# Compressed scores as transposed products, bias tables and sample rounds moved, all expert row dots from PSUM

## What is computed

```python
def dense_attn(q, k, v, q_pos, k_pos, slopes, window):
    s = jnp.einsum('...qgrd,...kgd->...grqk', q, k) * (B_HD ** -0.5)
    dist = q_pos[..., None, None, :, None] - k_pos[..., None, None, None, :]
    s = s - slopes[:, :, None, None] * dist
    p = jnp.where(mask, jax.nn.softmax(jnp.where(mask, s, NEG), axis=-1), 0.0)
    o = jnp.einsum('...grqk,...kgd->...qgrd', p, v)
    return o, p
...
    y_b = (g[:, :, 0] * o_cmp + g[:, :, 1] * o_slc + g[:, :, 2] * o_win)
...
def one(xb):                                   # peer_ffn, per token block
    ...
    top_s, j = lax.top_k(cand, P_TOPK)         # 8 heads, 16 of 16384 experts each
    eidx = jnp.take_along_axis(cidx, j, axis=-1)
    gate = jax.nn.softmax(top_s, axis=-1)
    u = peer_u[eidx]
    v = peer_v[eidx]
    act = jax.nn.gelu(jnp.einsum('td,tpkd->tpk', xb, u), approximate=False)
    return jnp.einsum('tpk,tpkd->td', gate * act, v)
```

## Time and profile before

| | us |
|---|---|
| median of 3 runs | 2270.77 |
| lowest and highest | 2267.69, 2270.86 |
| the profiled execution | 2268.58 |
| its span, first to last instruction | 2266.9 |

### The profile page before, as it was taken

How to read it: one execution, slowest core, us unless ns; L and a number is a source line. 1 busy time by engine, 2 the same in 40 slices (tenths; PEclk the granted TensorE clock), 3 DMA queues, 4 the chain that set the end, 5 groups by cost and what they waited for, 6 DMA issues and landing times.

```text
span 2266.9 us, 34232 instructions
## 1 busy us (share of the span) xinstructions
PE 2144.5 (95%) x13322; PEld 1893.3 (84%) x13322; DVE 1500.4 (66%) x3063; ACT 992.6 (44%) x1760; POOL 917.7 (40%) x608
## 2 busy tenths in 40 slices
PE   7999999988998999999989998999999999999998
PEld 7798988766555987999989998899997787888886
DVE  3334232345777545397889879975536989888886
ACT  2122322232777431333336665566543454454452
POOL 1000222311210000346866766677665554655530
PEclk9999999996999999999989999999999999999999
DMA  5234333346101543227879997999999999999993
GB/s 202 79 138 112 107 107 111 115 159 173 35 2 39 182 140 117 93 77 230 300 245 295 313 303 250 307 342 353 370 309 358 373 386 377 387 397 389 388 358 124
DMA packets 190233, 518.05 MB, mean 229 GB/s; under 512 B 15684, under 2 KB 85432, under 8 KB 185336
## 3 DMA queue, kind: packets, MB, share of 16 engines
q1 hardware_dynamic: 138648, 330.28, 41.7%
q0 software_dynamic: 50848, 184.53, 22.3%
q10 hardware_dynamic: 576, 1.05, 0.1%
HBM read 446.18 MB, written 73.75 MB: 229 GB/s over the span
## 4 chain that ended last, share of the span: by engine, by line
PE 46%; DVE 9%; DMA 3%; ACT 1%; issue 1%; SPq 0%; POOL 0%; DVEq 0%; ACTq 0%
PE ps_e L2439 22%; PE ps_e L2410 5%; PE ps_e L2411 5%; PE ps_e L2414 5%; DVE row L2760 3%; PE ps_e L2431 3%; DMA u_raw<-in_peer_uT 2%; PE ps_e L2463 1%; PE ps_e L2468 1%; PE ps_e L2469 1%; PE ps_e L2472 1%; PE ps_e L2399 1%; DMA e_gate<-gate_tables 1%; DVE one_a L2745 1%; DVE one_b L2745 1%
## 5 line engine op out<-in xcount | busy, mean ns | idle before, releaser
L2352 POOL DMA_INDIRECT row<-in_peer_v,sparse_idx x160 | 270.4, 1690 | 220.0 <-DVE y L2768 159.4
L2410 PE MATMUL ps_e<-hTh,u_hi 128*128 128x384 f32 x1024 | 358.1, 350 | 0.4 <-ACT gelu_out L2515 0.4
L2359 POOL TENSOR_TENSOR u_lo<-u_raw,u_hi 128x1024 fp32r<-128x1024 f32 x128 | 314.6, 2459 | 101.9 <-ACT u_hi L2509 99.1
L2411 PE MATMUL ps_e<-hTl,u_hi 128*128 128x384 f32 x1024 | 350.2, 342 | 0.0
L2439 PE MATMUL ps_e<-v_hi,w_hi 128*128 128x512 f32 x768 | 243.6, 399 | 5.5 <-DVE v_lo L2788 4.1
L2439 PE MATMUL ps_e<-v_lo,w_hi 128*128 128x512 f32 x768 | 241.5, 395 | 0.0
L2439 PE MATMUL ps_e<-v_hi,w_lo 128*128 128x512 f32 x768 | 241.4, 396 | 0.0
L2788 DVE TENSOR_TENSOR v_lo<-v_raw,v_hi 128x1024 fp32r<-128x1024 f32 x128 | 161.0, 1260 | 97.5 <-ACT v_hi L2548 97.5
L2414 PE MATMUL ps_e<-hTh,u_lo 128*128 128x384 f32 x1024 | 201.1, 338 | 0.5 <-POOL u_lo L2359 0.5
L2352 POOL DMA_INDIRECT row<-in_peer_u,sparse_idx x150 | 156.6, 1044 | 103.1 <-DVE sparse_hid L2760 79.7
L2410 PEld LDWEIGHTS ps_e<-hTh,u_hi 128*128 128x128 f32 x1024 | 196.8, 192 | 0.7 <-ACT u_hi L2509 0.7
(11 more groups left out here) (528 smaller groups left out, 4666.2 us busy)
## 6 DMA issues: line engine op xcount, KB each, us to landing
u_raw<-in_peer_uT SPq DMA_DIRECT2D x128, 512.0 KB
v_raw<-in_peer_v SPq DMA_DIRECT2D x32, 2048.0 KB, 10.2
hidden_gelu<-gelu_out SPq DMA_DIRECT2D x64, 384.0 KB
gate_tables<-g_buf SPq DMA_DIRECT2D x48, 512.0 KB
e_gate<-gate_tables SPq DMA_DIRECT2D x32, 768.0 KB, 13.1
gelu_in<-hidden_gelu SPq DMA_DIRECT2D x32, 768.0 KB, 16.2
w_raw<-in_w_tiles SPq DMA_DIRECT2D x45, 512.0 KB, 3.5
gw_raw<-in_merge_tiles SPq DMA_DIRECT2D x16, 512.0 KB, 4.4
```

Of the source, the lines that this page charges most:

```text
L2352: pool.indirect_dma_start(out=row[:, :], out_offset=None, in_=io.peer_u if i < U_END else io.peer_v, in_offset=bass.IndirectOffsetOnAxis(a ...
L2359: pool.tensor_tensor(u_lo[:, n % UB, :, :], u_raw[:, n % UB, :, :], u_hi[:, n % UB, :, :].bitcast(F32), ALU.subtract).then_inc(ul_done, 1)
L2410: pe.matmul(ps[:, n % 2, 0:TD], u_hi[:, n % UB, dc, :], hTh[:, dc, :], start=(dc == 0), stop=False)
L2411: pe.matmul(ps[:, n % 2, 0:TD], u_hi[:, n % UB, dc, :], hTl[:, dc, :], start=False, stop=False)
```

## The change

Attention. `dist`, the first two pairs' bias tables, `cdist` and `valid` are made by GpSimd in `stage_compress`, and the same lines go from `stage_attend`. The compressed scores are computed transposed: for each group g, 32 columns of a wider `kcB` (its two 8-key blocks and zeros) are the stationary operand and 512 queries move, two rounds (r) of four groups that write different partitions of bank 7; ScalarE copies the result to SBUF as `csT`, and TensorE transposes it back in four tiles. VectorE's softmax of them moves from units 0 and 1 to 1 and 2, the other small steps by a unit, and the gate terms behind `minima(0)`. Each sample item comes one pair earlier, and the splits of `Y_AT` come every second unit.

Experts. ScalarE copies `hp` into PSUM banks 4 and 5 at the end of round 57, SP then loads the 128 prompt tokens into the tile `hp`, ScalarE copies them back into the banks at the end of round 81, and all dots read PSUM. `row_due` is dealt out in three parts to fit.

```diff
@@ -1032,13 +1032,17 @@
...
-    s.kcB = at("kcB", 52960, [P, KV, 2, 8])
+    s.kcB = at("kcB", 14144, [P, 16 + KV * 32])
...
-    s.att = 36992
+    s.att = a0 = 36992
...
+    s.bias = at("abias", a0 + 512, [P, 2, 2, TP])
@@ -1106,6 +1110,24 @@
...
+
+            pool.iota(s.dist[:, :], pattern=[[-1, TP]], base=384, channel_multiplier=1,
+                      allow_small_or_imprecise_dtypes=True)
+
+            pool.iota(s.cdist[:, :, :], pattern=[[P, 4], [-CB, 8]], base=1 - CB, channel_multiplier=1,
+                      allow_small_or_imprecise_dtypes=True).then_inc(dist_made, 1)
+            pool.wait_ge(dist_made, 1)
+            pool.affine_select(out=s.dist[:, :], in_=s.dist[:, :], compare_op=ALU.is_ge, fill=BIG, base=384,
+                               pattern=[[-1, TP]], channel_multiplier=1).then_inc(dist_made, 1)
+            pool.affine_select(out=s.valid[:, :, :], in_=s.ones[:, 0:32].rearrange("p (i n) -> p i n", i=4),
+                               compare_op=ALU.is_ge, fill=0.0, base=1 - CB, pattern=[[P, 4], [-CB, 8]],
+                               channel_multiplier=1)
+            pool.affine_select(out=s.cdist[:, :, :], in_=s.cdist[:, :, :], compare_op=ALU.is_ge, fill=BIG, base=1 - CB,
+                               pattern=[[P, 4], [-CB, 8]], channel_multiplier=1)
+            pool.wait_ge(dist_made, 2)
+            for p in range(2):
+                for e in range(2):
+                    pool.tensor_scalar(s.bias[:, p, e, :], s.dist[:, :], SLOPES[2 * p + e], None, ALU.mult)
@@ -1179,8 +1201,9 @@
...
-            link(dve.tensor_scalar(s.kcB[0:HD, :, 0, :], src, pcol[0:HD, 0:1], None, ALU.add))
-            dve.tensor_copy(s.kcB[HD:P, :, 1, :], s.kcB[0:HD, :, 0, :])
+            keys = s.kcB[:, 16:16 + KV * 32].rearrange("p (g x) -> p g x", x=32)
+            link(dve.tensor_scalar(keys[0:HD, :, 0:8], src, pcol[0:HD, 0:1], None, ALU.add))
+            dve.tensor_copy(keys[HD:P, :, 8:16], keys[0:HD, :, 0:8])
@@ -1258,7 +1279,7 @@
...
-    items = [("p", 0), ("p", 1), ("p", 2), ("s", 0), ("p", 3), ("s", 1), ("p", 4), ("s", 2), ("p", 5), ("s", 3), ("p", 6), ("p", 7)]
+    items = [("p", 0), ("p", 1), ("s", 0), ("p", 2), ("s", 1), ("p", 3), ("s", 2), ("p", 4), ("s", 3), ("p", 5), ("p", 6), ("p", 7)]
@@ -1268,12 +1289,13 @@
...
-    Y_AT = [SMP_END + 4 + dc for dc in range(DC)]
+    Y_AT = [SMP_END + 4 + 2 * dc for dc in range(DC)]
...
+        chain = sem("att_chain")
...
+        csT_psum, csT_ready = sem("csT_psum"), sem("csT_ready")
@@ -1438,27 +1443,33 @@
...
             scores(1)
-            for i in range(4):
-                for p in range(NP):
-                    last = pe.matmul(ps[:, 7, i * P + 16 * p:i * P + 16 * (p + 1)], s.bqT[:, p, i * P:(i + 1) * P],
-                                     s.kcB[:, 2 * p // REP, :, :].rearrange("p e n -> p (e n)"), start=True, stop=True)
-            last.then_inc(cs_psum, 1)
+            for r in range(2):
+                for g in range(KV):
+                    c = 32 * g + 16 * (1 - r)
+                    last = pe.matmul(ps[32 * g:32 * g + 32, 7, :], s.kcB[:, c:c + 32], s.bqT[:, 2 * g + r, 0:TP],
+                                     start=(r == 0), stop=(r == 1))
+            last.then_inc(csT_psum, 1)
             for u in range(NU):
...
                     scores(u + 2)
+                if u == 0:
+                    pe.wait_ge(csT_ready, 1)
+                    for i in range(4):
+                        last = pe.transpose(ps[:, 7, i * P:(i + 1) * P], csT[:, i * P:(i + 1) * P], s.ident[:, :])
+                    last.then_inc(cs_psum, 1)
                 turn(u)
...
                         turn_rows(k)
-                if u == 3:
+                if u == 4:
                     pe.wait_ge(pc_ready, 1)
...
                     last.then_inc(pcT_psum, 1)
-                if u == 5:
+                if u == 6:
                     pe.wait_ge(sel_ready, 2)
@@ -1476,10 +1487,11 @@
...
-            dve.wait_ge(gate_exp, 1)
-            dve.tensor_scalar(s.gden[:, 0:4, :], s.gden[:, 0:4, :], 1.0, None, ALU.add)
-            dve.tensor_scalar(s.gden[0:TS, 4, :], s.gden[0:TS, 4, :], 1.0, None, ALU.add).then_inc(gden_ready, 1)
-            dve.wait_ge(gden_ready, 1)
+            def gate_terms():
+                dve.wait_ge(gate_exp, 1)
+                dve.tensor_scalar(s.gden[:, 0:4, :], s.gden[:, 0:4, :], 1.0, None, ALU.add)
+                dve.tensor_scalar(s.gden[0:TS, 4, :], s.gden[0:TS, 4, :], 1.0, None, ALU.add).then_inc(gden_ready, 1)
+                dve.wait_ge(gden_ready, 1)
@@ -1570,24 +1581,25 @@
...
             minima(0)
+            gate_terms()
             for u in range(NU):
...
                 scale(u)
-                if u == 0:
+                if u == 1:
                     compressed_scores()
-                if u == 1:
+                if u == 2:
                     compressed_shares()
...
                     masked_values(12, BH)
-                if u == 4:
+                if u == 5:
                     dve.wait_ge(pcT_psum, 1)
                     dve.tensor_copy(pcT[:, :], ps[:, 7, :]).then_inc(pcT_ready, 1)
-                if u == 5:
+                if u == 4:
                     masked_values(6, 12)
...
                     masked_values(0, 6).then_inc(vbd_ready, 1)
-                if u == 7:
+                if u == 8:
                     gate_sums()
@@ -1659,9 +1671,12 @@
...
                 exponentials(u)
+                if u == 0:
+                    act.wait_ge(csT_psum, 1)
+                    act.copy(csT[:, :], ps[:, 7, :]).then_inc(csT_ready, 1)
                 if u >= 1:
                     copy_turned(u - 1)
-                if u == 1:
+                if u == 2:
                     act.wait_ge(cexp_in, 1)
@@ -2173,8 +2188,11 @@
...
-    row_due = ([0] * PRE + [30 + i * 52 / 68 for i in range(68)]
-               + [82 + i * 36 / (U_END - PRE - 68) for i in range(U_END - PRE - 68)]
+    PACK_AT, H3_AT = 57, 81
+    LAST3 = HALF3 + NSP
+    row_due = ([0] * PRE + [30 + i * 25 / (HALF3 - PRE) for i in range(HALF3 - PRE)]
+               + [PACK_AT + 1 + i * 21 / NSP for i in range(NSP)]
+               + [H3_AT + 1 + i * 36 / (U_END - LAST3) for i in range(U_END - LAST3)]
@@ -2280,6 +2298,10 @@
...
                                  gbuf[b % 2][:, gs, :, :].rearrange("p g t j -> p g (t j)")).then_inc(g_sent[b % 2], 16)
+                if n == PACK_AT + 2:
+
+                    sp.wait_ge(h3_ready, 2)
+                    sp.dma_start(hp[:, :], io.h_rows[TD:TP, :]).then_inc(h3_in, 16)
                 if n == V_AT:
@@ -2622,6 +2644,14 @@
...
                     gate_copy(q)
+                if n == PACK_AT:
+                    act.wait_ge(hp_in, 16 * 4)
+                    act.wait_ge(rows_done, HALF3)
+                    act.copy(ps[:, 4:6, :], hp[:, :].rearrange("p (a b) -> p a b", a=2)).then_inc(h3_ready, 1)
+                if n == H3_AT:
+                    act.wait_ge(h3_in, 32)
+                    act.wait_ge(rows_done, LAST3)
+                    act.copy(ps[:, 4:6, :], hp[:, :].rearrange("p (a b) -> p a b", a=2)).then_inc(h3_ready, 1)
                 if n == GP_AT:
@@ -2755,9 +2785,10 @@
...
                     if i == HALF3:
-                        dve.wait_ge(hp_in, 16 * 4)
-                    token = ps[:, 4:6, :] if c < NS3 else hp[:, :].rearrange("p (a b) -> p a b", a=2)
-                    dve.tensor_tensor_reduce(out=row, in0=row, in1=token, scale=1.0, scalar=0.0, op0=ALU.mult,
+                        dve.wait_ge(h3_ready, 2)
+                    if i == LAST3:
+                        dve.wait_ge(h3_ready, 3)
+                    dve.tensor_tensor_reduce(out=row, in0=row, in1=ps[:, 4:6, :], scale=1.0, scalar=0.0, op0=ALU.mult,
                                              op1=ALU.add, accum_out=hid[:, c:c + 1]).then_inc(rows_done, 1)
...
                 dve.wait_ge(rows_done, i)
```

## The result

| us | before | after |
|---|---|---|
| median, lowest to highest (5 runs each) | 2270.77, 2267.04 to 2273.63 | 2256.99, 2245.25 to 2262.66 |
| ratio of the two, 95% interval | | 0.9938, 0.9909 to 0.9966 |
| the profiled execution, its span | 2268.58, 2266.9 | 2256.99, 2255.3 |

The kernel is faster by 13.8 us (0.6%). The forecast was 2252.0 with a range of 2240 to 2262. A second set of 12 runs of the same kernel, between fresh runs of before, gave 0.9953 (0.9937 to 0.9969), 11.8 us. So the gain fell short of the forecast 18.8 by 5 to 7 us; the median lies inside the stated range and 1 us above the 2248 to 2256 that the forecast called its own.

What follows compares the result with a forecast made beforehand. TensorE was taken as the bound, so edits pay only where it stands still or runs at low clock. Terms -7.0 - 2.0 - 9.8 = -18.8 us gave 2249.8 profiled, median 2252.0; range 2240 to 2262.

Steps and rivals of the forecast that it cites:

- Attention start: Start of the attention stage: early tables and transposed compressed scores bring the first turned tile forward, -7.0 us.
- the clock term: Attention start: 1.2 GHz lasting until 561 gives back up to 5 of 7.4 us; -7.0 taken.
- the bound of 10: Attention start: upper bound of the gain, -10 us, used for the clock rising early.
- the first rival: Attention start: the low clock eats the gain, -2.5 in place of -7.0 us, total 2256.5; chance 0.17.
- The second rival: Clock rises early at attention start (-10), wait near rounds 58 to 62 mostly goes (-7, with its clock): 2241; chance 0.15.
- Sample rounds: End of the attention stage: sample items a pair earlier let the splits spread, -2.0 us (bounds +1 and -5.3).
- at the earlier rate it would idle 1.8: Last 39 us of attention: TensorE idles 7.1 us, 1.8 at the earlier rate; less than half of 5.3 counted.
- First standstill: Expert hidden loop, rounds 58 to 62: VectorE ends `resolve` sooner with short dots, -2.6 us; half clock stays.
- Second standstill: Expert hidden loop, `resolve` of round 79: VectorE's lead covers it, -5.3 us, and -2.9 for the half clock.
- barrier: PSUM refills after rounds 57 and 81 drain the row pipeline: 2276 for both (chance 0.04), 2264 for one (0.05).
- DMA behind round 82: Rounds 82 to 118: three more rows, 1.6 MB, cost +1.0 us (bounds 0 and +4.4).
- the rival on DMA: From round 82 DMA takes over: +4.4 us and one more standstill with half clock (4.7 + 2.9), 2263; chance 0.08.

Runs made afterwards that it cites:

- part 3 alone: Kernel before with only the expert change (PSUM refills, all row dots from PSUM, new due rounds): 2257.86 us, ratio 0.9958.
- part 1 alone: Kernel before with only the transposed compressed scores and the early bias tables, items and splits as before: 2256.82 us, ratio 0.9952.

## Why the prediction was right, and which steps were not

The measured 13.8 us lie in the range partly because errors cancelled. By the stages of the two traces, attention gained 8.3 us where 9.0 were forecast (both parts), rounds 57 to 66 5.1 for 2.6, rounds 66 to 82 8.5 for 8.2, but rounds 82 to 127 lost 6.2 for 1.0 and rounds 30 to 57 4.3 for nothing.

**Attention start: right mechanism, gain too small, since the clock term was mis-sized.** From the timelines, with the time at 1.2 GHz in windows of half a microsecond:

| | first score to first turned tile | at 1.2 GHz near the start | attention stage |
|---|---|---|---|
| before | 15.5 | 27.3 | 204.2 |
| early tables alone | 15.3 | 27.3 | 203.1 |
| transposed scores alone | 7.6 | 17.1 | 196.8 |
| both (alone on before) | 5.4 | 13.7 | 193.6 |
| after | 5.4 | 13.7 | 195.9 |

The forecast put the first turned tile 7.1 us behind the start, with products and transposes at the half clock, and took another 0.4 to 1.4 us off for a low clock that lasts; the bound of 10 stood for the case in which it returns early. That case came: the level was back at 539.5, behind the 3.57 us of dense streaming, so scores(2) and the transposes already ran at full speed. (It isn't always so quick: in the trace of after without the sample rounds the first spell lasts 6.8 us.) A second spell of 10.2 us comes with the gap in front of 547.11, and then none up to 697, where the clock is 1.00 in the window above. Both halves are needed, as the forecast said of the tables (hidden as long as TensorE is late): alone they are worth 1 us in the trace, no more than traces of the same attention code differ by, behind the shorter product 3.2 (196.8 to 193.6). Note the trap: the first rival, that the clock eats the gain, gave 2256.5, the measured number to half a microsecond, and its mechanism is refuted. The number alone would have taught the wrong thing. (The second rival, which had the early clock and a first standstill that shrinks with its clock, was right in part; its 2241 comes out of its own terms as 2244.6, unless the clock's share is counted on top.)

**Sample rounds: wrong.** The failed step is "at the earlier rate it would idle 1.8": it took the idling of the last 39 us for the work of the splits. With the splits spread TensorE idles 8.0 us instead of 8.7 before the merge's first product. Beside part 1 the whole stage is 0.4 to 2.3 us longer with the new sample rounds (195.9, 195.1 and 195.2) than without them (193.6, 194.7, 193.7 and 193.8); without part 1 the traces don't part them (205.6, and 205.2 for the order alone, against 204.2, 204.2 and 205.2). The times say 0.2, 0.6 and 2.2 thousandths against them. One cost that the forecast didn't look for stands behind the stage: from the merge's first product to round 0 four of the five traces with the new item order take 299.8 to 299.9 us and the fifth 298.8, while eight of the nine with the old order take 297.6 to 298.1 and the ninth 298.7. The version with the order alone is among the four (299.8), so the order is enough for it; its cause was not looked into. So the sample rounds gain nothing; whether they cost 0 or 5 us in all the times don't tell.

**First standstill: right, a little small.** Rounds 57 to 66 took 5.1 us less, forecast was 2.6 with the half clock staying. TensorE's long wait fell from 9.1 to 4.7 us, and the spell at 1.2 GHz behind it from 10.2 to 3.4 us, of which the forecast counted nothing.

**Second standstill: right.** Rounds 66 to 82 took 8.5 us less, forecast was 8.2; 9.2 and 8.1 in two other traces with these due rounds, but 0.9 in the one whose slab load came late in round 70. In after the refills were no barrier: their copies take 1.02 us each, VectorE waited once for the second (3.5 us, in the row under the dots above), and TensorE's waits for `u_lo` between 1320 and 1470 us are 0.5 us in all. With the refill at the end of round 78, just before the `resolve` of round 79, one does hold VectorE up, in all three traces with the old due rounds; in that of after with the old due rounds:

```profile
1434.11 1.02 ACT L2653 COPY ps_e<-h_pack 128x1024 f32<-128x1024 f32 x1
1435.27 1.22 DVE L2790 CUSTOM_DVE_ANT_0 row<-row,ps_e 128x1024 f32<-128x1024 f32 x1 [6.56 <-issue]
```

VectorE starts when the copy is out, and TensorE waits 2.6 us in round 81.

**DMA behind round 82: mis-sized.** Forecast +1.0 with an upper bound of 4.4; rounds 82 to 127 took 6.2 us more. Waits from 1480 to 1660 us, in before, in after and in the last version with the old due rounds:

```profile
ACT u_hi L2509 <- DMA u_raw<-in_peer_uT: 16.0, 8, 6.2
...
PE ps_e L2431 <- ACT one_b L2522: 6.3, 4, 4.9
```

```profile
ACT u_hi L2531 <- DMA u_raw<-in_peer_uT: 26.3, 14, 8.2
...
PE ps_e L2453 <- ACT one_b L2544: 11.8, 4, 6.9
```

```profile
ACT u_hi L2530 <- DMA u_raw<-in_peer_uT: 19.3, 13, 6.5
...
PE ps_e L2452 <- ACT one_b L2543: 7.4, 4, 5.2
```

The third wait of TensorE is put down to the one-hots, but the chain through the hole at 1620 shows what was late, in after:

```profile
1607.42 14.85 DMA u_raw<-in_peer_uT
1622.30 1.04 ACT u_hi L2531
1623.35 1.19 ACT one_b L2544 x4
1624.58 2.08 PE ps_e L2453 x8
```

A slab load is 14.85 us under way, ScalarE waits for it with the cast, and the one-hots that it must scale stand behind that cast. Before, the same link is 12.79 us long:

```profile
1622.06 12.79 DMA u_raw<-in_peer_uT
```

The 395 GB/s of 1610 to 1630, which the forecast held against this, was read just before that hole. Over the traces TensorE idles 10.5 to 12.0 us in rounds 82 to 127 with short dots and new due rounds (four traces) and 6.5 to 9.3 in the ten others, and waits 5.8 to 6.9 us in round 111 against 4.3 to 5.9. The sum had priced 1.6 MB more at the DMA rate and left out the hole and its half clock, which the rival on DMA had: the clock is 0.97 on the mean from 1480 to 1660 instead of 0.99. Why three rows more should lengthen the loads so much was not isolated. The Trainium skill, DMA: Bandwidth & Descriptors, section on queues, rings and completion order, says that each DMA engine takes turns between its queues a packet at a time, which fits a slab load stretched by gathers on another queue; no run here varied that alone.

**Rounds 30 to 57: not costed.** The forecast looked at no effect of the new rows there, as their rate is the old one. With dots from PSUM and new due rounds they took 154.0, 154.5, 154.1 and 152.1 us, in four traces; with the old due rounds 148.4, 150.1 and 149.6; before 149.7; new due rounds and dots from SBUF, 147.9. The sum over these rounds also holds other small holes (in the five other traces with the loop of before it is 148.2 to 152.0), so the stretch alone doesn't prove it; three of its rounds do. Rounds 51 to 53 take 19.7 us in three of the four traces with short dots and new due rounds, 18.1 in the fourth, and 15.3 in all ten others. The place is the `resolve` of round 51, a chain of long VectorE steps with two inputs in SBUF. In after, and in the last version with the old due rounds:

```profile
1274.69 4.38 DVE L2726 TENSOR_TENSOR oh<-partf,i 128x2048 f32<-128x2048 f32 x1
1279.10 4.56 DVE L2731 TENSOR_TENSOR oh<-oh,idxf 128x1024 f32<-128x1024 f32 x2
...
1286.02 1.22 DVE L2750 TENSOR_TENSOR res<-top 128x128 f32<-128x128 f32 x1
```

```profile
1273.90 2.29 DVE L2725 TENSOR_TENSOR oh<-partf,i 128x2048 f32<-128x2048 f32 x1
1276.22 4.43 DVE L2730 TENSOR_TENSOR oh<-oh,idxf 128x1024 f32<-128x1024 f32 x2
...
1280.69 2.29 DVE L2732 TENSOR_REDUCE res<-oh 128x128 f32<-128x2048 f32 x1
```

In the first of the two, GpSimd's subtraction has just begun when the step comes; in the second it comes later, and it is the one that is slow:

```profile
1274.49 2.43 POOL L2381 TENSOR_TENSOR u_lo<-u_raw,u_hi 128x1024 fp32r<-128x1024 f32 x1 [0.48 <-ACT u_hi L2531]
```

```profile
1274.72 3.71 POOL L2380 TENSOR_TENSOR u_lo<-u_raw,u_hi 128x1024 fp32r<-128x1024 f32 x1 [1.61 <-ACT u_hi L2530]
```

One step takes 4.38 instead of 2.29 us, in the three other traces the pair behind it 6.6 instead of 4.4: one more collision of 2.1 to 2.2 us with a `u_lo`, the same effect as in the row dots. (By the rule of the Trainium skill quoted in the prediction they lock each other out; these pairs agree.) Behind it TensorE waits 2.5 us and the clock is down for 3.4 us, where before and with the old due rounds there is no wait at all between 1280 and 1310. The change took 32 operations out of that conflict and left the resolves in it, and where VectorE meets GpSimd has moved, by less than 1 us: in the four traces that collide `u_lo` begins between 0.2 us before and 0.2 behind the first long step, in before and in the three with short dots and old due rounds 0.8 us behind it, in the one with new due rounds and long dots 0.5. The collision is there in all four traces that have both the short dots and the new due rounds and in none of the ten others. What sets this meeting was not isolated.

The hidden loop in all 14 traces, us:

| | 30-57 | 57-66 | 66-82 | 82-127 | sum |
|---|---|---|---|---|---|
| before | 149.7 | 62.7 | 93.8 | 234.8 | 541.0 |
| its loop in five other versions | 148.2-152.0 | 61.6-62.5 | 93.7-93.8 | 234.0-236.8 | 540.3-544.8 |
| new due rounds, dots from SBUF | 147.9 | 62.4 | 101.0 | 237.4 | 548.7 |
| dots, refills, new due rounds | 154.1 | 57.5 | 85.7 | 240.4 | 537.8 |
| after | 154.0 | 57.6 | 85.3 | 241.0 | 537.9 |
| after, again | 154.5 | 57.3 | 84.6 | 240.8 | 537.3 |
| after without the sample rounds (late slab load) | 152.1 | 58.8 | 92.9 | 242.0 | 545.8 |
| after with old due rounds | 150.1 | 56.6 | 89.4 | 233.7 | 529.8 |
| old due rounds, no sample rounds | 148.4 | 56.3 | 89.1 | 235.3 | 529.1 |
| the same, again | 149.6 | 56.4 | 89.5 | 236.0 | 531.5 |

So the dots from PSUM gain 9 to 12 us in the loop with the old due rounds. The new ones, leaving out the trace with the late slab load, bring 4 us more from 66 to 82, where the refill no longer stands in front of a `resolve`, and give back 4 from 30 to 57 and 5 to 6 behind 82. Due rounds and refills move together in these edits, so the runs don't part the two. This is where the missing 5 to 7 us of the forecast are: 18.8 was forecast, 16 to 19.5 are measured with the old due rounds.

**What stays open.** Parts 1 and 3 alone gave 10.9 and 9.5 us by the ratios, 20 together (18 by the medians), and the whole 12 to 14. The stretches of the traces don't show an interaction: the loop of part 3 alone is as long as that of after (537.8 and 537.9), the attention stage of part 1 alone within 2.4 us. But the traced execution of part 3 alone was the slowest of its nine (2264.65, median 2257.86), so its trace can't say where its faster runs gained. By the intervals the sum of the two parts is known to about 5 us and the whole to 4 to 6.5, so whether the parts add up is open.

## What to carry to other kernels

A slow instruction that loses its conflict, or a wait that is taken away, only pays up to the next thing in the queue. Here the operand moved to PSUM did what was forecast to the digit (1.21 us, 150 of 150), and the schedule dealt out anew around it gave 5 to 6 us of it back behind round 82, where the DMA share was 1.00 before, and 4 at a `resolve`, against 4 that it gained elsewhere. Change one of the two at a time, and count a clock spell with the hole that opens or closes: the holes of 3 to 9 us in this loop each came with one of 3.4 to 10.2 us, those of 2.5 to 3 us some of the time. Compare two traces by rounds and not by the time on the axis: a hole that seems new may have stood 12 us later before. And keep the trace that doesn't fit. And when a predicted number comes out, read the profile for the mechanism all the same: the rival that hit it was the wrong one.

## What was not expected of the hardware

- The 1.2 GHz level ended 3.4 us after it had begun, with the 3.57 us of 512-column products, whose weights are 32 columns wide; in 13.75 us of 16-column products with full weight loads, listed as busy throughout, it stayed down, 27.3 us in all. In another trace with the new products it ended after 6.8 us.
- 16 instructions of 128*32 with 512 columns, on four groups of columns, took 3.34 to 3.57 us with part of them at the half clock: the four groups run side by side. One after another the eight products would take 9 us at the full clock, at 1.12 us for one (two instructions).
- Runs of one kernel spread by 17 us between the lowest and highest of 5 after the change and by 6.6 before, in the first comparison; in the later ones runs of before (23 and 24) spread by 14 to 19 us and 12 of after by 13, so a wider spread after the change is not shown. Which of VectorE's long steps meets a `u_lo` differs from trace to trace of the same kernel (the first step in one of after's two traces, the third in the other), at 2.1 to 2.2 us each.
